# Gate panels among head norms, rotation and turns; a delta-rule pair's norm inside the next pair's levels

## The reference

```python
(fq, fk, fv, ff, dq, dk, dv, iq, ik, iw, mq, g) = jnp.split(u @ w_in[l], SPLIT_POINTS, axis=-1)
o_a = fox_attention(rmsnorm(fq), rmsnorm(fk), fv, logf)          # 8 heads, forget gate
o_b = dsa_attention(rope(rmsnorm(dq)), rope(rmsnorm(dk)), dv, rope(iq), rope(ik), iw, k_sel)   # top-k keys
o_c = memory_attention(rmsnorm(mq), km, vm)                      # 4 heads, 256 memory tokens
gates = jax.nn.sigmoid(g.reshape(B, S, N_BRANCHES, D))
h = h + jnp.sum(gates * proj, axis=2) @ w_out[l]
```

```python
sol = lax.linalg.triangular_solve(lmat, rhs, left_side=True, lower=True, unit_diagonal=True)
o_a = gdn_chunked(q, k, v, g, beta)
o_a = rms_norm(o_a, gdn_norm_w) * jax.nn.silu(z_a.reshape(bsz, s, GDN_HEADS, GDN_DV))
```

## Time and profile before

| | |
|---|---|
| median of three runs | 2552.12 us |
| the profiled execution's own time | 2547.68 us |
| its span | 2545.9 us |
| TensorE busy (matmuls) | 2433.0 us, 96% |
| VectorE busy | 1340.0 us, 53% |
| ScalarE busy | 886.6 us, 35% |
| POOL busy | 120.5 us, 5% |
| weight traffic in a stage of plain projections | 95 GB/s |

### The profile page before, as it was taken

How to read it: one execution, slowest core, us unless ns; L and a number is a source line. 1 busy time by engine, 2 the same in 40 slices (tenths; PEclk the granted TensorE clock), 3 DMA queues, 4 the chain that set the end, 5 groups by cost and what they waited for, 6 DMA issues and landing times.

```text
span 2545.9 us, 31666 instructions
## 1 busy us (share of the span) xinstructions
PE 2433.0 (96%) x12764; PEld 1902.3 (75%) x12764; DVE 1340.0 (53%) x2037; ACT 886.6 (35%) x1480; POOL 120.5 (5%) x156
## 2 busy tenths in 40 slices
PE   7999999997999999999999999788998999999997
PEld 6888888885566668888888767677876687788886
DVE  5454335435467537644543486334464754777623
ACT  4222223321344444422222454343346243433321
POOL 0000000000022220000000000223100000000000
PEclk9999999997999999999999999888998999999998
DMA  5333324320122115333332332000021232233331
GB/s 167 99 93 97 97 79 136 105 75 9 46 63 66 51 58 175 100 99 95 96 100 84 83 83 81 12 1 2 25 77 42 58 93 73 84 98 100 96 97 48
DMA packets 372465, 200.02 MB, mean 79 GB/s; under 512 B 12000, under 2 KB 364512, under 8 KB 372320
## 3 DMA queue, kind: packets, MB, share of 16 engines
q1 hardware_dynamic: 372320, 198.01, 26.9%
HBM read 190.38 MB, written 7.60 MB: 78 GB/s over the span
## 4 chain that ended last, share of the span: by engine, by line
PE 90%; DVE 6%; ACT 2%; issue 1%; DMA 0%; POOL 0%; DVEq 0%; SPq 0%; ACTq 0%
PE ps L516 19%; PE ps L517 19%; PE ps L518 19%; PE ps L376 2%; PE ps L1011 2%; PE ps L1418 2%; PE ps L1420 2%; PE ps L1419 2%; PE ps L378 2%; PE ps L377 2%; PE ps L1047 2%; PE ps L2122 1%; PE ps L2124 1%; PE ps L2123 1%; PE ps L898 1%; PE ps L764 1%
## 5 line engine op out<-in xcount | busy, mean ns | idle before, releaser
L449 DVE TENSOR_TENSOR w_lo<-w_raw,w_hi 128x1024 fp32r<-128x1024 f32 (+2 forms) x366 | 422.8, 1156 | 308.7 <-ACT w_hi L465 307.5
L516 PE MATMUL ps<-u_hi,w_hi 128*128 128x512 f32 (+1 forms) x1416 | 556.1, 393 | 3.0 <-DVE w_lo L449 2.1
L517 PE MATMUL ps<-u_lo,w_hi 128*128 128x512 f32 (+1 forms) x1416 | 553.6, 391 | 0.0
L518 PE MATMUL ps<-u_hi,w_lo 128*128 128x512 f32 (+1 forms) x1416 | 553.5, 391 | 0.0
L465 ACT ACTIVATE w_hi<-w_raw 128x1024 fp32r<-128x1024 f32 (+2 forms) x366 | 366.3, 1002 | 467.1 <-PE ps L518 438.3
L516 PEld LDWEIGHTS ps<-u_hi,w_hi 128*128 128x128 f32 (+1 forms) x1416 | 263.7, 186 | 64.2 <-DVE w_lo L449 3.0
L517 PEld LDWEIGHTS ps<-u_lo,w_hi 128*128 128x128 f32 (+1 forms) x1416 | 263.6, 186 | 60.2 <-issue 2.0
L518 PEld LDWEIGHTS ps<-u_hi,w_lo 128*128 128x128 f32 (+1 forms) x1416 | 263.5, 186 | 59.4 <-issue 0.8
L518 PE MATMUL ps<-mid_hi,w_lo 128*128 128x512 f32 x528 | 208.6, 395 | 0.0
L517 PE MATMUL ps<-mid_lo,w_hi 128*128 128x512 f32 x528 | 208.6, 395 | 0.0
L516 PE MATMUL ps<-mid_hi,w_hi 128*128 128x512 f32 x528 | 208.6, 395 | 0.0
(11 more groups left out here) (440 smaller groups left out, 3691.1 us busy)
## 6 DMA issues: line engine op xcount, KB each, us to landing
w_raw<-w_in_dram SPq DMA_DIRECT2D x101, 512.0 KB, 3.8
w_raw<-ffn_w_gate_dram SPq DMA_DIRECT2D x44, 512.0 KB, 3.8
w_raw<-ffn_w_up_dram SPq DMA_DIRECT2D x44, 512.0 KB, 3.8
w_raw<-w_up_dram SPq DMA_DIRECT2D x44, 512.0 KB, 3.8
w_raw<-ffn_w_down_dram SPq DMA_DIRECT2D x32, 512.0 KB, 4.0
w_raw<-w_out_dram SPq DMA_DIRECT2D x24, 512.0 KB, 3.9
w_raw<-w_down_dram SPq DMA_DIRECT2D x16, 512.0 KB, 3.8
w_raw<-ffn_w_down_dram SPq DMA_DIRECT2D x16, 384.0 KB, 3.4
```

The lines of the kernel that those rows point to most:

```text
L449: dve.tensor_tensor(lo, raw, hi.bitcast(F32), ALU.subtract).then_inc(w_split, 1)
L516: pe.matmul(out, wh, h_k, start=k0 + k == 0, stop=False)
L517: pe.matmul(out, wh, l_k, start=False, stop=False)
L518: mm = pe.matmul(out, wl, h_k, start=False, stop=end)
```

## The change

Four gate panels move from attention to the stages ahead of the indexer. `squares_pe` of the last batch feeds one block before each of its four sums; `block_norms_pe` feeds six before it waits for the inverses; `rotate_pe` feeds two behind each of ten matmuls; `token_pe` feeds one ahead of entries 3 and 6. The indexer keeps its 40 blocks. In attention the jobs 0 to 11, 12, 14 and 16 feed a panel each. ScalarE's and VectorE's shares (upper, lower, keep) move with them. The first nine panels rotate over the four banks; from the tenth on, bank 3 alone is used, as before.

In the delta-rule heads the stages `ss`, `rt`, `inv`, `bk`, `out` of a pair are walked inside the next pair's levels: `ss` behind `u` of level 1, `rt` behind `t` of level 1, `inv` behind `u` of level 2, `bk` behind `u` of level 3, `out` behind `u` of level 4. The next pair's `bc` waits for `sq` and its `w` for `out`. The squares go to another tile, sums and spread to bank 3 of the head.

```diff
     def gate_bank(m):
-        return ps[2 if m in (1, 3) else 3][:, :]
+        return ps[(segs["gates"].group + m) % BANKS if m <= 8 else 3][:, :]
...
-            pe.wait_ge(bank_read, s.group + BANKS + (m - 1 if 1 <= m < 5 else m))
+            pe.wait_ge(bank_read, s.group + m + (1 if m <= 8 else BANKS))
...
+    FED = tuple(range(12)) + (12, 14, 16)
+    def fed_panel(n):
+        return 9 + FED.index(n)
...
-    def squares_pe(pe, blocks, batch, sq, mm):
+    def squares_pe(pe, blocks, batch, sq, mm, panels=None):
         for i, e in enumerate(batch[1], batch[0]):
+            if panels:
+                feed(panels, 1)
...
-    def block_norms_pe(pe, blocks, inv, bc, done):
+    def block_norms_pe(pe, blocks, inv, bc, done, panels=()):
+        feed(panels, 6)
         pe.wait_ge(inv, 1)
...
             pe.matmul(ps[4 + e % 2][0:rows, :], cst[0:rows, C_ROT:C_ROT + rows], x, start=True, stop=True).then_inc(rope_mm, 1)
+            feed(panels, 2)
...
+            if e == 5:
+                gate_keep_dve(dve, 1)
...
         for e in range(10):
+            if e in (3, 6):
+                feed(panels, 1)
...
         for n in range(NJ):
+            blocks = 4 if n in FED else 0
             scores(n, (3, 2))
             if n:
                 turn(n - 1, (1, 0))
-            feed(panels, 4)
+            feed(panels, blocks)
...
-            if n + 5 < GATES:
-                gate_upper(act, n + 5)
+            if n in FED:
+                gate_upper(act, fed_panel(n))
...
+    PE_STAGES = behind(["bc", "kk", "t0"] + lev + ["w"] + scan, (("u", 1), "ss"), (("u", 3), "bk"))
+    ACT_STAGES = behind(["dec", "small", "t0"] + [x for x in lev if x[0] != "u"] + ["w"] + [("v", c) for c in range(QB)] + ["sq"],
+                        (("t", 1), "rt"))
+    DVE_STAGES = behind(["kb", "at", "qk"] + [("u", l) for l in range(NL - 1)] + ["full", ("u", NL - 1)] + [("s", c) for c in range(QB)],
+                        (("u", 2), "inv"), (("u", 4), "out"))
...
+    NEXT_PAIR = ("ss", "rt", "inv", "bk", "out")
+    TURNS = {eng: [(stage, n) for pair in range(5) for stage in stages
+                   for n in (2 * pair, 2 * pair + 1) for n in (n - 2 if stage in NEXT_PAIR else n,) if 0 <= n < 8]
+             for eng, stages in STAGES.items()}
...
                 if n >= 2:
-                    pe.wait_ge(g_dve, after("dve", "out", n - 2))
+                    pe.wait_ge(g_act, after("act", "sq", n - 2))
...
             elif stage == "w":
+                if n >= 2:
+                    pe.wait_ge(g_dve, after("dve", "out", n - 2))
...
-                x = act.activation(X, B[2][:, :], ACT.Square)
+                x = act.activation(upper(n), B[2][:, :], ACT.Square)
...
@@ scalar
             roots_act(act, head_norms, head_mm, head_rt, root, HEAD_ROOTS)
+            gate_upper(act, 0)
...
             act.activation(cosT, turns_f, ACT.Sin, scale=-1.0).then_inc(trig, 1)
+            for m in (1, 2, 3):
+                gate_upper(act, m)
...
@@ vector
+            gate_lower(dve, 0)
             block_norms_dve(dve, head_norms, head_rt, len(HEAD_ROOTS), root, head_inv, head_bc, head_done)
+            gate_keep_dve(dve, 0)
             rotate_dve(dve, st)
+            gate_keep_dve(dve, 2)
+            for m in (1, 2, 3):
+                gate_lower(dve, m)
             dve.wait_ge(token_done, 12)
+            gate_keep_dve(dve, 3)
```

More of the change, by code:

```diff
@@ L816, in angles_dve, with rotate_pe @@
         dve.sem_inc(trig, 1)
-    def rotate_pe(pe):
+    def rotate_pe(pe, panels):
         for e, (x, rows) in enumerate(rotated):
@@ L1124, in attend_dve @@
                 e = QB * n + DOWN.index(q)
-                if q == 3:
-                    gate_keep_dve(dve, n + 4)
+                if q == 3 and (n == 0 or n - 1 in FED):
+                    gate_keep_dve(dve, fed_panel(n - 1) if n else 8)
                 dve.wait_ge(sc_mm, e + 1)
@@ L1496, in build, with behind, heads_in_turn @@
     scan = [(k, c) for c in range(QB) for k in ("v", "s")]
-    PE_STAGES = ["bc", "kk", "t0"] + lev + ["w"] + scan + ["ss", "bk"]
-    ACT_STAGES = ["dec", "small", "t0"] + [x for x in lev if x[0] != "u"] + ["w"] + [("v", c) for c in range(QB)] + ["sq", "rt"]
-    DVE_STAGES = ["kb", "at", "qk"] + [("u", l) for l in range(NL - 1)] + ["full", ("u", NL - 1)] + [("s", c) for c in range(QB)] + ["inv", "out"]
+    def behind(stages, *later):
+        out = []
+        for stage in stages:
+            out += [stage] + [x for spot, x in later if spot == stage]
+        return out
+    PE_STAGES = behind(["bc", "kk", "t0"] + lev + ["w"] + scan, (("u", 1), "ss"), (("u", 3), "bk"))
[3 more added lines that the diff above has]
+                        (("u", 2), "inv"), (("u", 4), "out"))
     POOL_STAGES = ["q", "vb"] + [("c", l) for l in range(NL - 1)] + ["kbe", "kd"]
     STAGES = {"pe": PE_STAGES, "act": ACT_STAGES, "dve": DVE_STAGES, "pool": POOL_STAGES}
+    NEXT_PAIR = ("ss", "rt", "inv", "bk", "out")
+    TURNS = {eng: [(stage, n) for pair in range(5) for stage in stages
+                   for n in (2 * pair, 2 * pair + 1) for n in (n - 2 if stage in NEXT_PAIR else n,) if 0 <= n < 8]
+             for eng, stages in STAGES.items()}
+    PLACE = {(eng, stage, n): i + 1 for eng, turns in TURNS.items() for i, (stage, n) in enumerate(turns)}
     def after(eng, stage, n):
-        order_ = STAGES[eng]
-        return n // 2 * 2 * len(order_) + 2 * order_.index(stage) + n % 2 + 1
+        return PLACE[eng, stage, n]
     def slots(n):
         return [solve_t[:, n % 2, k, :] for k in range(6)]
[L1512 to L1516, removed]
+    def heads_in_turn(eng):
+        for stage, n in TURNS[eng]:
+            yield stage, stage[0] if isinstance(stage, tuple) else stage, n
     def packed(x, half):
@@ L1532, in gdn_pool @@
     def gdn_pool(pool):
-        for stage, what, n in heads_in_turn(POOL_STAGES):
+        for stage, what, n in heads_in_turn("pool"):
             vb, kt = chunks(qkv[:, 16 + n, :]), chunks(ktok[:, n, :])
@@ L1561, in gdn_pe @@
     def gdn_pe(pe):
-        for stage, what, n in heads_in_turn(PE_STAGES):
+        for stage, what, n in heads_in_turn("pe"):
             At, Tm, U, X, C, QK = slots(n)
@@ L1640, in gdn_pe @@
                 for c in range(QB):
-                    mm = pe.matmul(B[0][:, c:c + 1], X[:, cc[c]], ones[:, 0:1], start=True, stop=True)
+                    mm = pe.matmul(B[3][:, c:c + 1], upper(n)[:, cc[c]], ones[:, 0:1], start=True, stop=True)
             elif stage == "bk":
                 pe.wait_ge(g_dve, after("dve", "inv", n))
-                mm = spread(pe, B[1], stat[:, 48 + 4 * (n % 2):52 + 4 * (n % 2)], QB)
+                mm = spread(pe, B[3], stat[:, 48 + 4 * (n % 2):52 + 4 * (n % 2)], QB)
             mm.then_inc(g_pe, 1)
     def gdn_act(act):
-        for stage, what, n in heads_in_turn(ACT_STAGES):
+        for stage, what, n in heads_in_turn("act"):
             At, Tm, U, X, C, QK = slots(n)
@@ L1687, in gdn_act @@
                     o = 40 + 4 * (n % 2) + c
-                    x = act.activation(stat[:, o:o + 1], B[0][:, c:c + 1], ACT.Sqrt, bias=QEPS[:, c, n:n + 1], scale=1.0 / 128)
+                    x = act.activation(stat[:, o:o + 1], B[3][:, c:c + 1], ACT.Sqrt, bias=QEPS[:, c, n:n + 1], scale=1.0 / 128)
             x.then_inc(g_act, 1)
     def gdn_dve(dve, st):
-        for stage, what, n in heads_in_turn(DVE_STAGES):
+        for stage, what, n in heads_in_turn("dve"):
             At, Tm, U, X, C, QK = slots(n)
```

22 lines of the change are left out of this document (11 added, 11 removed).

## The result

The changed kernel takes 2534.57 us, the median of four runs (2534.4 to 2539.1), against 2552.11 for the kernel before: ratio 0.9938, interval 0.9923 to 0.9954, or 16 us less (12 to 20). Five more runs on another chip gave 2534.88 and 0.9930 (0.9915 to 0.9946). The forecast was 2537.4 in 2527 to 2548. The profiled execution took 2534.51 us, its span is 2532.7.

A forecast was written before the change was run, and what follows sets the result against it. TensorE holds 90% of the chain and bounds attention. Panels -19.7 us and norm +5 sum to -14.7, so 2533.0 from the profiled 2547.7; plus 4.4 for the median, 2537.4 us, range 2527 to 2548.

The forecast's parts named there:

- Attention: Attention jobs: four more without a panel save 5.5 us each, less 1.2 for VectorE's splits: -20.8 us.
- Rival 1: Attention: unfed jobs bound by the softmax chain, not TensorE, saving 3 us instead of 5.5: 2547 us; chance 0.14.
- Squares and norms: Ahead of the rotation: spread begins 1.6 us later, first 48 spreads regain 2.6 at high clock: net -1.0 us.
- Rotation: Before the turns: ten entries become TensorE-bound, 2.62 us instead of 2.18: +4.4, less 0.5 at the last.
- Rival 3: Rotation runs at the low clock, entries near 4.9 us, +23 there, total +8: 2560 us; chance 0.06.
- Indexer: Indexer's first 10 us, low-clocked before, give back 0 to 4.4 us at full clock; middle taken, -2.2 us.
- Boundaries: Between delta-rule pairs: the serial tail goes, the exponential's table reloads at two: -6.5, -5.3, -6.6, sum -18.4 us.
- Levels: Delta-rule levels: sums 1.75, roots 2.3, inverses nothing, spread 1.6, products 1.5; 7.15 us a pair, +21.5 for three.
- The clock: Delta-rule levels: an idle or thin stretch may lower the clock, 2 to 3 us a pair; 2 us added in all.
- Rival 2: Levels hide the norm: half of 21.5 us in gaps gives 2524 us, all hidden 2516; chance 0.10.
- Rival 4: ScalarE pauses 1.4 us at each of five table changes in levels and path, +7: 2544 us; chance 0.03.
- Rival 5: Delta-rule levels at half clock in each pair, the norm's part near +14 us: 2547 us; chance 0.05.

The follow-up runs named there:

- experiment 1: Only the gate panels moved, delta-rule stages left as in the kernel before: 2534.54 us, ratio 0.9927 against the kernel before.
- experiment 5: Changed kernel with the whole norm moved to the gap ahead of the next pair's levels, spread and products early: 2519.17 us, ratio 0.9875 against the kernel before.
- experiment 2: Only the norm moved into the next pair's levels, gate panels as in the kernel before: 2554.17 us, ratio 1.0010 against the kernel before.
- experiment 8: Changed kernel with no blocks between the last squares and all ten behind them: 2539.5 us, ratio 0.9961 against the kernel before.

## Why the prediction was right

It was right in total (2537.4 against 2534.6) and in the sign of both parts: -19.7 against -18.6 (15 to 22) for the panels, +5 against +2.6 (0.5 to 4.9) for the norm. Part of that agreement is luck: in each part terms missed in opposite directions. Step by step:

- *Attention, -20.8:* 20.8 in every trace. The unfed jobs run at 7.61 us, so four of them give 4 x 5.37 = 21.5; the 1.2 us charged for VectorE's splits was not measured by itself. TensorE's wait for POOL in attention is 2.3 us in three times, as in the earlier trace rows. Rival 1 is out.
- *Squares and norms, -1.0:* -0.7 in the first profile (rotation from 607.6 to 606.9), +4.4 where the clock fell (612.0). "If the extra blocks keep the clock up" was the right condition, but I took it as met. It was met in two of eight traces, so the term was mostly a loss of about 4 us and not a gain of 1. What balanced it is the next term, charged too high.
- *Rotation, +3.9 for its ten entries:* too high. They and the wait behind them took 24.3 us to the first turn instead of 23.1: +1.2. The 2.62 us came from an indexer turn with a score of 64 rows. With a rotation matmul of 128 rows an entry takes 2.25 us, with one of 64 rows 2.49. A row that resembles the moved work in its shape, not only in its column count, would have been the one to look for. Rival 3 is out: the clock is back at 1.00 before the rotation in every trace with the moved panels, and the ten entries take the same 24.3 us in those where the squares were slow.
- *Turns, +0.4:* 631.1 to 639.1, 8.0 instead of 8.2: -0.25.
- *Indexer, -2.2 as the middle of 0 and -4.4:* -1.4 (60.55 us instead of 61.91). The clock was carried through the turns, and was lost just behind them. In two other traces of the same code (experiments 1 and 5) the low stretch was longer and the indexer took 62.0 us, no gain.
- *Boundaries, -6.5, -5.3 and -6.6:* 6.6, 5.3 and 6.6 by the table.
- *Levels, 7.15 a pair:* in the second pair (5.65 - 3.69) + (6.52 - 3.69) + (5.92 - 3.69) + (3.98 - 3.72) = 7.3. The terms: sums 1.96 (1.75 forecast), roots 2.8 (2.3; the low clock of this level, which is there without the roots too, is in it), spread 2.2 (1.6), products 0.26 (1.5, the one term that failed: VectorE's 2.70 us of copies were busy, as I read them, but only because two of the four run beside POOL; put behind the products they take 1.46). The 7.3 meets the 7.15 because this term is 1.2 too high and the others together 1.4 too low. In the fourth pair level 1 too runs at half clock in part, 6.60.
- *The clock, +2:* by the medians 0.4 is left for it (2.6 + 18.5 - 20.7); it is low against this pair of traces, where the stretches ahead of the levels and the first pair add 7.5 us. But part of that is not the norm's. The kernel with the panels alone has the delta-rule code of before, and its first two pairs take 33.99 and 33.63 us from the keys to `w` where the profile of before shows 32.08 and 32.21 (its level 1 takes 4.88 us in the first pair instead of 3.75, and the second pair 9.99 instead of 8.44 ahead of level 0). The profiled execution of before is 4.4 us faster than its median, which the prediction added; such stretches are likely where, which no run shows. Against the trace with the panels alone the norm costs 5.5, not 9.8.
- Rival 2 (the levels hide the norm) is out by every level of the table. Rival 4 is out: the table follows the copy ahead of it by 0.02 us, and the root starts 0.01 us behind the table (1658.61). Rival 5's mechanism is there in part: stretches at 0.50 around the roots, but near 7 us long in each pair and not the whole of the levels.
- Two small sums in the recorded text are off: "all hidden" in rival 2 gives 2514 us by its own terms, not 2516, and the chances listed for "faster" add up to 0.83, not 0.81. The forecast doesn't hang on either.

The Trainium skill, "ScalarE: Activation LUTs", section "What ACT_TABLE_LOAD costs", counts a drain of about 1380 ns to every switch beside the load. No run here shows it, neither ahead of the load nor behind it; for the load itself its 1283 ns and the rows agree.

Experiments 2 and 5 answer what the sum could only say in one number: the norm in the levels was worse than the tail by 2.6 us, and in the gap better by 13 (0.9875 with the panels, against 0.9927 for the panels alone; the intervals lie apart). Both save the same 18.5 us of boundary. The difference lies in what the moved pieces meet: the roots met a copy for which TensorE waited, in the gap they met a wait.

Open: why the medians give the norm's cost as 2.6 and the nearest traces as 5.5; why the clock falls behind the squares in one execution and not in another; and where the kernel of experiment 8 loses 6 to 8 us.

## What to carry to other kernels

- Filling a stage in which TensorE waits pays one for one, if the stage from which the work comes is bound by TensorE: find both in the waits, then move whole panels. A serial tail moved into a full loop comes back as the sum of its pieces; look for the stretch where the engine that the loop waits for is idle, and price each place by what is queued behind the moved instruction.
- Take the price of a moved instruction from a row with the same shape and the same neighbour, and look at the single instructions of a group: four equal copies took 1.02, 1.04, 0.28 and 0.29 us here, and what stood beside them made the difference. An instruction put ahead of them can be nearly free if it moves them away from that neighbour.
- Before two traces are subtracted, set each against the median of its kernel. One lucky execution on one side was worth 4 us here, and led to an expectation 9 us off.

## What the hardware showed

- VectorE's copy of 64x256 in float32 takes 0.28 to 0.29 us with POOL idle, and 0.86 to 1.10 when POOL multiplies beside all of it or 85% and more, in all eleven traces. VectorE's product of 128x512 with one operand in PSUM takes 0.75 us in both cases.
- The same code at the same place ran at 1.00 in one execution and at 0.50 in another: squares of 0.95 or 1.70 us a group, 5 us in the whole. The two traced executions of the changed kernel differ by 5.1 us; its nine times spread over 10 us (2529.6 to 2539.6), and seven of them have no trace to say why.
- A level that is not stretched takes 3.69 us whether its rows show 1.15 (norm in the gap), 1.22 or 1.38 us each (spread back in the levels, at a granted clock of 1.00). These lengths hold waits between the two heads, so a group's length says little of TensorE's work.
- An entry of the rotation with a matmul of 64 rows among matmuls of 128 takes about 0.25 us more than one with 128 rows throughout (2.49 against 2.25). Whether the change of rows or the matmul itself costs this isn't shown.
